# Block two of a fused two-block transformer: x is transposed unscaled, and the norm's scale is applied to the projections instead

## What is computed

```python
# end of the first block, then the start of the second
x = rmsnorm(x + peer(...), final_norm_g)
h = rms_norm(x, norm_g)                      # x * rsqrt(mean(x*x)) * g
proj = h @ w_in                              # 1024 -> 4648 columns
q, k, v, qi, ki, wi, z_a, u_b, z_b, gates = split(proj)
a = dsa_attention(rope(norm(q)), rope(norm(k)), v, rope(qi), rope(ki), wi, k_sel) * silu(z_a)
b = multiscale_pool(u_b, pool_w, pool_scale) * silu(z_b)   # trailing means over 2, 4, 8, 16 tokens
g = sigmoid(gates + merge_bias)
y = g[:, :, 0] * (a @ w_branch_a) + g[:, :, 1] * (b @ w_branch_b)
x = x + y @ w_out
```

## Time and profile before

| what | us |
|---|---|
| median of three runs | 1963.4 (1961.99 to 1964.46) |
| the profiled execution, its own time | 1961.98 |
| its span, first to last instruction | 1960.6 |

### The profile page before, as it was taken

How to read it: one execution, slowest core, us unless ns; L and a number is a source line. 1 busy time by engine, 2 the same in 40 slices (tenths; PEclk the granted TensorE clock), 3 DMA queues, 4 the chain that set the end, 5 groups by cost and what they waited for, 6 DMA issues and landing times.

```text
span 1960.6 us, 23683 instructions
## 1 busy us (share of the span) xinstructions
PE 1946.6 (99%) x9095; PEld 1594.0 (81%) x9095; DVE 1196.8 (61%) x2165; ACT 715.8 (37%) x1028; POOL 920.4 (47%) x637
## 2 busy tenths in 40 slices
PE   8999999999999999999999999999999999999999
PEld 7777888888888778888888888888888888777787
DVE  4454542499999662222223688888888874895344
ACT  3335432332333343222223333333333335635452
POOL 1000000007878888888871777776787500720000
PEclk9999999999999999999999999999999999999999
DMA  7543423146666659666667899999999913331122
GB/s 272 186 145 116 158 99 117 60 146 145 146 145 146 134 125 273 145 143 149 146 165 265 278 374 370 377 353 367 356 380 358 389 67 97 86 97 54 50 91 86
DMA packets 183568, 375.23 MB, mean 191 GB/s; under 512 B 61792, under 2 KB 101216, under 8 KB 175008
## 3 DMA queue, kind: packets, MB, share of 16 engines
q1 hardware_dynamic: 109264, 277.03, 41.6%
q0 software_dynamic: 68976, 86.53, 16.9%
q10 hardware_dynamic: 5216, 10.16, 1.5%
HBM read 312.64 MB, written 60.97 MB: 191 GB/s over the span
## 4 chain that ended last, share of the span: by engine, by line
PE 96%; DVE 3%; ACT 1%; issue 1%; DMA 0%; ACTq 0%; DVEq 0%
PE bank L1619 36%; PE bank L328 18%; PE bank L330 18%; PE bank L329 18%; PE bank L2300 1%; PE bank L1216 1%; DVE x L1887 1%; PE bank L2280 1%; PE bank L550 1%; PE bank L1499 1%; DVE v_low L1876 1%; PE bank L2289 1%; PE bank L604 0%; PE bank L570 0%; PE bank L615 0%
## 5 line engine op out<-in xcount | busy, mean ns | idle before, releaser
L1453 POOL DMA_INDIRECT gates_scratch<-slot_gate,slot_place x256 | 434.7, 1698 | 293.9 <-DVE slot_place L1410 205.6
L1619 PE MATMUL bank<-xn_low,u_high 128*128 128x512 f32 x1024 | 403.1, 394 | 0.0
L1619 PE MATMUL bank<-xn_high,u_high 128*128 128x512 f32 x1024 | 398.8, 389 | 0.0
L1619 PE MATMUL bank<-xn_high,u_low 128*128 128x512 f32 x1024 | 398.6, 389 | 0.0
L1671 DVE TENSOR_TENSOR u_low<-u_raw,u_high 128x1024 fp32r<-128x1024 f32 x128 | 156.5, 1223 | 284.6 <-ACT u_high L1642 284.2
L328 PE MATMUL bank<-v_high,w_high 128*128 128x512 f32 x768 | 298.9, 389 | 0.2 <-DVE v_low L1876 0.2
L330 PE MATMUL bank<-v_high,w_low 128*128 128x512 f32 x768 | 298.8, 389 | 0.0
L329 PE MATMUL bank<-v_low,w_high 128*128 128x512 f32 x768 | 298.8, 389 | 0.0
L321 DVE TENSOR_TENSOR weights_low<-weights_raw,weights_high 128x1024 fp32r<-128x1024 f32 (+1 forms) x105 | 127.6, 1217 | 221.6 <-ACT weights_high L310 221.5
L1658 ACT ACTIVATE hidden<-bank 128x512 f32<-128x512 f32 x128 | 76.5, 598 | 419.7 <-PE bank L1619 415.7
L1619 PEld LDWEIGHTS bank<-xn_high,u_high 128*128 128x128 f32 x1024 | 192.2, 188 | 40.4
(11 more groups left out here) (343 smaller groups left out, 3045.5 us busy)
## 6 DMA issues: line engine op xcount, KB each, us to landing
u_raw<-in_peer_u SPq DMA_DIRECT2D x128, 512.0 KB, 4.1
v_raw<-in_peer_v SPq DMA_DIRECT2D x64, 1024.0 KB, 8.3
weights_raw<-in_w_in SPq DMA_DIRECT2D x62, 512.0 KB, 3.7
hidden_scratch<-hidden SPq DMA_DIRECT2D x128, 192.0 KB
hidden_in<-hidden_scratch SPq DMA_DIRECT2D x32, 768.0 KB, 11.5
gates_scratch<-nothing POOLq DMA_DIRECT2D x32, 576.0 KB, 3.0
gate_in<-gates_scratch SPq DMA_DIRECT2D x32, 576.0 KB, 7.2
weights_raw<-in_w_out SPq DMA_DIRECT2D x16, 512.0 KB, 3.7
```

Of the source, the lines that this page charges most:

```text
L1453: pool.engine.indirect_dma_start(gates, bass.IndirectOffsetOnAxis(p.slot_place[t][:, i:i + 1], 0), p.slot_gate[t][:, i:i + 1], None, compu ...
L1619: step = pe.engine.matmul(m.bank[b][:, :], left[:, k, :], right[:, k, :], start=(done == 0), stop=(done == 3 * KT - 1))
```

## The change

In block two PE transposes x by a plain transpose against the identity, k by k, with no scale in it. The sums of squares of t0 to t2 stay where they were; those of t3, the mean, the root and the reciprocal for all four tiles come behind the eight evictions of h, on ACT and on DVE. The scale is applied later:

- `kv`, `index`, `z_a`, `q` (token major): ACT takes the scale of the tile as the scale operand of the eviction; DVE's copy of the index keys and weights (`kiw`) becomes a multiplication from the bank.
- `u_b`, `z_b` and the gates: ACT evicts them plainly, and GpSimd multiplies each 128x512 part by a row of scales, `scale_row_two`, which it makes once by `row_by_dram` (two DMAs). It does the four parts of u_b ahead of the index sums, the four of z_b behind them and ahead of the trailing means, and the sixteen of the gates behind the means, each as it is evicted. Silu of z_b becomes an in-place step of ACT in `mixing`. The sigmoids wait for GpSimd.

```diff
-        (self.tables_two_arrived, ...
+        self.rows_moved, self.pool_scaled = semaphores(nc, "rows_moved pool_scaled")
...
-MADE = {"kv": 0, "index": 4, "u_b": 8, "z_b": 12, "z_a": 16, "q": 20}
+MADE = {"kv": 0, "index": 4, "z_a": 8, "q": 12, "z_b": 16}
+BY_ROW = {"u_b": 0, "z_b": 4, "gate": 8}
...
 def two_pool(m, w):
+    pool.wait_ge(s.norm_scale, SCALES_LAST)
+    row_by_dram(m, 1, w.gained[3], w.scale_row, 2 + 2 * PACKS)
+    pool.wait_ge(s.scale_row_ready, 32)
+
+    def scale_rows(name, rows):
+        for i in range(4):
+            pool.wait_ge(s.rows_moved, BY_ROW[name] + i + 1)
+            pool.engine.tensor_tensor(rows[:, i, :], rows[:, i, :], w.scale_row[:, :], ALU.mult).then_inc(s.pool_scaled, 1)
+
     pool.wait_ge(s.turned_low, 4 * KT)
     pool.wait_ge(s.tables_two_arrived, 16 * TABLES)
+    scale_rows("u_b", w.pooled)
     for t in range(2, TT):
...
-    pool.wait_ge(s.made, MADE["u_b"] + 4)
+    scale_rows("z_b", w.mixed)
+    pool.wait_ge(s.pool_scaled, BY_ROW["u_b"] + 4)
...
+    for half in range(2):
+        for branch in range(2):
+            for i in range(4):
+                part = w.gate[half][branch][:, i, :]
+                pool.wait_ge(s.gate_moved, 8 * half + 4 * branch + i + 1)
+                pool.engine.tensor_tensor(part, part, w.scale_row[:, :], ALU.mult).then_inc(s.pool_scaled, 1)
...
 def two_tensor(m, keep, w, combining):
-    def turn(t, columns):
-        pe.wait_ge(s.scales_spread, TT + t + 1)
-        for k in columns:
-            ...
-            step = pe.engine.matmul(m.bank[b][:, t * P:t * P + P], keep.x[:, t, k * P:k * P + P], w.spread[:, t, :],
-                                    start=True, stop=True)
-    for columns in (range(TURN_FIRST), range(TURN_FIRST, KT)):
-        for t in range(TT - 1):
-            turn(t, columns)
-    turn(TT - 1, range(KT))
+    for k in range(KT):
+        b = TURN_BANKS[k]
+        m.await_bank(b)
+        for t in range(TT):
+            pe.wait_ge(*outputs_added(m, k // 4, t))
+            step = pe.engine.transpose(m.bank[b][:, t * P:t * P + P], keep.x[:, t, k * P:k * P + P], ident)
+        step.then_inc(s.turned, 1)
+        m.bank_freed[b] = (s.turned_low, 3 * KT + k + 1)
...
 def two_scalar(m, keep, w, combining):
+    for n in range(2 * TT - 2):
+        square(n // 2, n % 2)
...
         act.engine.activation(w.h_high[:, k, :], m.bank[TURN_BANKS[k]][:, :], ACT.Copy, scale=w.both_gains[:, k:k + 1]).then_inc(s.turned_high, 1)
+    square(TT - 1, 0)
+    square(TT - 1, 1)
+    rms_scalar(m, NORM_LAST, w.gained[2][:, :])
     act.wait_ge(s.turned_low, 4 * KT)
     rms_scalar(m, NORM_RESIDUAL, w.last[2][:, :])
+    act.wait_ge(s.norm_scale, SCALES_LAST)
...
-            act.engine.activation(tensor[:, i, :], bank[:, 0:width], func).then_inc(s.made, 1)
+            act.engine.activation(tensor[:, i, :], bank[:, 0:width], func, scale=w.gained[3][:, i:i + 1]).then_inc(s.made, 1)
...
     def mixing():
         for g in range(4):
+            act.wait_ge(s.pool_scaled, BY_ROW["z_b"] + g + 1)
+            act.engine.activation(w.mixed[:, g, :], w.mixed[:, g, :], ACT.Silu).then_inc(s.made, 1)
             yield 0.7
...
     def open_gates():
-        act.wait_ge(s.gate_moved, 16)
+        act.wait_ge(s.pool_scaled, BY_ROW["gate"] + 16)
```

More of the change, by code:

```diff
@@ L1411, in place, with row_by_dram @@
         dve.wait_ge(s.gates_placed, t + 1)
-def row_by_dram(m, n, scale, row):
+def row_by_dram(m, n, scale, row, relaid):
     pool, s = m.pool, m.s
@@ L2022, in __init__ @@
         early = Region(nc, p.scores_at)
-        self.spread = early.tensor("spread_two", [P, TT, P], F32)
+        early.at += T * 4
         self.squares = [early.tensor(f"squares{i}", [P, BANK], F32) for i in range(4)]
@@ L2378, in square @@
         n = 2 * t + half
-        next(combining)
+        next(combining, None)
         act.wait_ge(*outputs_added(m, half, t))
@@ L2521, in two_scalar @@
     spare = [0.0]
-    gather("u_b", w.pooled, between(spare, choosing, choosing, choosing))
+    gather_rows("u_b", w.pooled, between(spare, choosing, choosing, choosing))
     act.step(act.engine.activation(w.small[:, 3, 63:64], keep.ident[:, 0:1], ACT.Silu))
-    gather("z_b", w.mixed, between(spare, choosing), ACT.Silu)
+    gather_rows("z_b", w.mixed, between(spare, choosing))
     gather("z_a", w.z_a, between(spare, choosing), ACT.Silu)
@@ L2644, in gain @@
                                scalar=0.0, op0=ALU.mult, op1=ALU.add, accum_out=w.gained[0][:, n:n + 1]).then_inc(s.gained_squared, 1)
[L2646 to L2664 removed]
     for n in range(2 * TT):
         next(combining)
[L2668 to L2670 removed]
+        if 0 < n < 2 * TT - 1:
             gain(n - 1)
[L2672 to L2676 removed]
     for _ in combining:
         pass
[L2679 to L2681 removed]
     for k in range(KT):
@@ L2685, in two_vector @@
                                in1=w.h_high[:, k, :].bitcast(F32), op0=ALU.mult, op1=ALU.subtract).then_inc(s.turned_low, 1)
+    gain(2 * TT - 2)
+    gain(2 * TT - 1)
+    dve.wait_ge(s.gained_squared, 2 * TT)
+    for halves, total, scratch, scale in (w.last, w.gained):
+        sums = halves.rearrange("p (t h) -> p t h", h=2)
+        dve.step(v.tensor_tensor(total, sums[:, :, 0], sums[:, :, 1], ALU.add))
+    dve.settle()
+    dve.step(v.tensor_scalar(w.last[2][:, :], w.last[1][:, :], RMS_EPS / D, RMS_EPS * RMS_EPS, ALU.mult, ALU.add))
+    dve.settle()
+    v.scalar_tensor_tensor(out=w.gained[2][:, :], in0=w.gained[1][:, :], scalar=1.0 / D, in1=w.last[2][:, :],
+                           op0=ALU.mult, op1=ALU.add).then_inc(s.norm_mean, 1)
+    dve.wait_ge(s.norm_root, NORM_LAST)
+    v.reciprocal(w.gained[3][:, :], w.gained[2][:, :]).then_inc(s.norm_scale, 1)
     dve.step(rms_vector(m, NORM_RESIDUAL, w.last[1][:, :], w.last[2][:, :], w.last[3][:, :], D))
@@ L2696, in move_keys @@
         dve.wait_ge(s.made, MADE["index"] + i + 1)
-        v.tensor_copy(w.kiw[:, i, :], m.bank[BANKS_OF["index"][i]][:, QUERIES:QUERIES + COLUMNS]).then_inc(s.kiw_moved, 1)
+        dve.wait_ge(s.norm_scale, SCALES_LAST)
+        v.tensor_scalar(w.kiw[:, i, :], m.bank[BANKS_OF["index"][i]][:, QUERIES:QUERIES + COLUMNS], w.gained[3][:, i:i + 1], None,
+                        ALU.mult).then_inc(s.kiw_moved, 1)
     scaling = residual()
```

67 lines of the change are left out of this document (14 added, 53 removed).

## The result

| | before | after |
|---|---|---|
| median, us | 1962.96 (1961.99 to 1964.46) | 1968.17 (1967.70 to 1970.10) |
| the profiled execution, us | 1961.98 | 1967.70 |
| its span, us | 1960.6 | 1966.4 |

A forecast was written before the change was run, and what follows sets the result against it. PE bounds the kernel (96% of the chain of waits), with 11.2 us at the handover to block two. Terms: -6.4 + 0.3 (u_b) + 0.2 (gates) = -5.9 us, so 1957.5 us; range for 8 in 10: 1955.6 to 1961.0.

The forecast's parts named there:

- Transposes and h: Handover to block two: 32 plain transposes take 3.34 us, kv never waits for `h_low`, PE gains 6.4 us.
- What is late next: DVE's scale chain behind h: the fourth chunk's low part is ready at 1617.2, 2.7 us early, at no cost.
- The row of scales: Two DMAs hold GpSimd from 1610.9 to 1632, hidden by over 20 us before u_b needs the row.
- the 0.1 of the bound: ACT evictions with a scale operand cost nil, bounded by 0.1 us on engines that wait for PE anyway.
- u_b: GpSimd products ahead of the index sums: DVE's sums of t1 grow 1 to 2.4 us; 0.3 reaches PE (0 to 0.9).
- one of the prediction's signs of being wrong: In the profile after, a gap of PE at the index scores would show the prediction wrong.
- slack of 1.5 us behind the sums: Behind DVE's sums of t1, 1.5 us of growth is absorbed before PE's next scores are delayed.
- The price per product: A two-input DVE step grows by 0.3 to 0.8 us for each GpSimd product it meets.
- slow rival: GpSimd blocks DVE in full at t1's sums (3.9 us) and attention (up to 15.5): 1975.4 us; chance 0.04.
- z_b: Four GpSimd products, 5.2 us, ahead of the means; PE wants the last mean later, so hidden by 9 us.
- The gates: Sixteen GpSimd products, 20.6 us: sigmoids at worst 0.7 us later, hidden; DVE's attention steps cost 0.2 (0 to 0.8).
- Two numbers of the rivals: Transposes not shorter, 0.213 us per fp32 product (chance 0.03); gain partly given back, 3 us lost, 1960.5 (chance 0.11).

The follow-up runs named there:

- e1: The changed kernel with its 24 GpSimd products (u_b, z_b, gates) cut to the first column of each part; 1956.25 us.
- e3: The changed kernel with GpSimd's products of the gates begun only when all four tiles of q are rotated; 1962.38 us.
- e5: The changed kernel with the planner's 5.5 us of projections ahead of PE's turn of q made 12.0; 1968.30 us.
- e2: e1 with the four products of the first quarter of the gates whole again; 1961.61 us.
- e4: e3 with the four products of u_b also moved behind the index sums; nothing left out; 1958.25 us.
- e10: e3 with the products of u_b and z_b cut to their first column, those of the gates whole; 1956.84 us.
- e9: The changed kernel with only the four products of u_b moved behind the index sums; 1964.27 us.
- e8: e2 with GpSimd multiplying each part by the constant 1.0 (one tensor operand) instead of the row of scales; 1957.42 us.

## Why the prediction was wrong

*Transposes and h: right.* 6.28 us at the second bank of kv instead of 6.4, 3.41 us for the 32 transposes (0.107 each) where 3.34 were forecast, no wait of PE for `h_low`. In e1 the same gain is still there at the turn of q (149.27 against 155.54, 6.27 us) and at the end.

*What is late next: right.* The fourth chunk's low part came at 1617.27, forecast 1617.2; this execution started 0.8 us later. The row of scales held GpSimd for 10.08 us and was there when the first product wanted it (that product, at 1651.62, waited for ACT's eviction). The evictions with a scale operand are 0.69 us instead of 0.60 (z_a, q) on an ACT that waits for PE, the 0.1 of the bound.

*u_b: the term of the sum that failed first.* Forecast were 1 to 2.4 us of growth over three products, of which 0.3 would reach PE (0 to 0.9). Measured were 3.9 us of growth (2.8 in the sums beside three products, 1.1 in the copy ahead of them, which the forecast passed over) and 2.4 us of waits of PE, a gap at the index scores, which was one of the prediction's signs of being wrong. So the slack of 1.5 us behind the sums was right, and the growth was not; the first index sum, said to start within 0.5 us of 1658, started at 1661.70. The time is 3.9 to 4.1 us by the medians. In the profiled execution, where the clock held, it is 2.6 at the t2 sum (92.65 against 90.09); with the fall of the clock that e3 and e5 show it is 4.1. The price per product was read from two rows, a low part 0.3 us and an addition 0.8 us over their neighbours, as if they were growth factors. But a step that met only the rest of a GpSimd instruction shows only a part of the price: the addition, 1.22 us in the earlier trace rows, lasts 0.43 in e1 and 1.40 beside the products of z_b. Where both engines have two-input steps one behind the other, every DVE step is held up by most of a product of 1.29 us: 0.93 us for each product at the sums of t1, 1.08 at the gains, 1.05 on the rotation's steps in e2. The prediction had a price of this kind, 3 x 1.29 = 3.9 us, in its slow rival, and gave the rival 0.04 because low parts had grown by 0.1 us on the mean in 60 us of GpSimd's work (1.32 us for 1.22). The low parts have two inputs too, but each stood alone between steps of the key choice, whose MAX8 and MATCH_REPLACE8 never grew (0.56 and 0.54 us on 128x384, beside products and without), and part of GpSimd's steps there have one operand or come after a pause. So that mean says little on two-input steps that follow one another on both engines.

*z_b: the cover was looked for on the wrong engine.* The means had their 9 us of slack, as forecast. But the eight products of u_b and z_b beside DVE's key choice lengthen it: in e4 the stretch from the t2 sum to the first mixing step is 45.33 us, in e1 44.06, and in front of it the scaling of t2's total takes 1.38 us instead of e1's 0.28. Of these 2.4 us on the way to q 1.0 is the time by which q was ready ahead of PE in e1. The time: 1.4 us (e4 less e10).

*The gates: 0.2 forecast, 6.0 measured.* The prediction looked at the attention, half 1 and the sigmoids, and passed over the first quarter, whose parts are evicted from 1753.40 on before, while DVE multiplies q by its gains from 1751.05 to 1753.54 and rotates it until 1755.8. It never asked who waits for q: PE's turn at 1757.28, 1.5 us later. That slack was in the trace, without a wait and so in no list of waits.

*The clock was no term at all.* Behind PE's wait for q it was at 0.50 of full speed. From the turn of q to the end the kernels that leave the turn at its place and have no wait, or with one of 1.2 or 1.6 us, take 203.3 to 203.6 us; with 3.03, 5.93 and 5.42 us of wait they take 205.0, 206.0 and 206.4. So 1.6 to 3.0 us come on top of those waits. The clock accounts for it: in e2 it is at 0.66 over the 5 us from 1755, 1.7 us lost, and in e9 at 0.51 over the 6.2 us behind the wait, 3.0 us lost.

The arithmetic for the changed kernel, from the table: PE's turn of q is 157.90 instead of 155.54 behind the start, 2.36 us late. That is the gain of 6.3 taken back by 8.6: 3.65 us at the t2 sum (92.65 against e1's 89.00), 1.6 in the choice of keys (45.70 against 44.06), 4.3 at the gains, less the 1.0 us by which q was ready ahead of PE in e1. With 2.66 us for the longer way to the end, the clock's part, this is 5.0 us, and the medians say 5.2.

The slow rival's mechanism is what happened, at 11.9 us lost in all, just over the 10.3 from which it was said to decide. But its places were wrong: it put 15.5 us on twelve products inside the attention, and these cost next to nothing (e10); one group of four cost half of the loss.

Two numbers of the rivals do not follow from the rows, and nothing hangs on them: an fp32 product against the diagonal is 0.23 us by the earlier trace rows (52 rows, two a product, in 6.07 us) and not 0.213, and 3 us lost of a gain of 6.4 is 1960.0 and not 1960.5.

The Trainium skill (SBUF — State Buffer, "Who interferes with whom") states that a DVE instruction with two SBUF inputs contends with a GpSimd instruction that reads SBUF, for ports that only one of them holds at a time. With two tensor operands on GpSimd the traces agree: 1.37 to 1.48 us for steps of 0.42. With one operand they show little of it: beside the TENSOR_SCALAR of e8, which reads SBUF too, the rotation lost 0.7 us over two of GpSimd's instructions of 1.70, and the measurement decides.

## What to carry to other kernels

An operation that moves to an idle engine is priced at whom it meets, not at its own length: lay its start and end, shifted, over the timeline of every engine that shares something with it, step by step. For each step that it can delay, find the slack of whoever reads the result, by the distance from its end to the reader's start; a distance of 1.5 us appears in no list of waits. And where two such steps alternate, the price is most of the neighbour each time (here 0.9 to 1.1 of 1.29 us), which a mean over mixed work hides. A wait of PE is then priced with the clock behind it: here the slow stretch added 1.6 to 3.0 us to waits of 3 to 6 us.

## What the runs showed of the hardware

- Two-input steps of DVE and GpSimd on SBUF tensors alternate: four DVE multiplications of 128x512 took 6.82 us beside four GpSimd products, 2.49 alone, while the products took 1.6 us each instead of 1.3. A DVE copy of 128x128 took 1.32 us for 0.22 and a TENSOR_SCALAR of 128x256 1.37 for 0.28 (e1) beside them; the key choice's MAX8 and MATCH_REPLACE8 were not touched.
- A PE wait of 5.93 us was followed by 3.6 us at a granted clock of 0.50 and 4 us at 0.81. Behind waits of 2.0 us at the same instruction the clock stayed at 1.00 in one execution (the changed kernel's) and was at 0.66 over some 5 us in two others (e3, e5).
- A plain fp32 transpose of 128x128 costs 0.107 us of PE (32 in 3.41 us), about half of the fp32 product against a diagonal matrix (0.23 us by the earlier trace rows).
- A scale operand from SBUF adds 0.09 us to an ACT eviction of 128x512 (0.69 for 0.60).
